# Reading expert rows back in another order at the end of a mixture-of-experts layer: picks 6 and 7 first, all tiles' sums begun with them, two pairs of rows moved from TensorE to VectorE

## The reference

```python
idx, gates = route(xf, w_router, router_bias)        # 8 of 64 experts for each of 640 tokens
hb = silu(xb @ w_gate[e]) * (xb @ w_up[e])           # for each block of rows of one expert
rows = hb @ w_down[e]
routed = segment_sum(rows * row_gate[:, None], row_tok)   # 8 gated rows summed for each token
x = x + gate * (routed + shared)                     # gate: a vector of width 1024 (g2)
y = rms_norm(x, norm_f)
```

## Time and profile before

| | us |
|---|---|
| median of 3 runs (lowest, highest) | 1039.57 (1038.82, 1041.35) |
| the profiled execution, its own time | 1040.67 |
| its span in the trace | 1038.9 |
| PE busy | 999.5 |
| DVE busy | 335.5 |
| ACT busy | 229.7 |
| POOL busy | 161.5 |
| mean rate of DMA over the span | 310 GB/s |

### The profile page before, as it was taken

One profiled execution on the slowest core, in us unless ns is written; L12 is line 12 of the kernel. 1 busy time (PEld: TensorE's weight loads), 2 busy tenths in 40 slices (PEclk: granted clock), 3 DMA queues, 4 the chain that ended last, 5 costly groups with the idle time before them and its releaser, 6 DMA issues.

```text
span 1038.9 us, 17717 instructions
## 1 busy us (share of the span) xinstructions
PE 999.5 (96%) x7077; PEld 446.7 (43%) x7077; DVE 335.5 (32%) x850; ACT 229.7 (22%) x547; POOL 161.5 (16%) x233
## 2 busy tenths in 40 slices
PE   6999999999999999999999999899999999999996
PEld 4435556565455553443333333333333333433342
DVE  1022225765236772322111111111121111112397
ACT  2131105665123240112111111111121111112111
POOL 1000010300131022112212112212122211121000
PEclk9999999999999999999999999999999999999998
DMA  9984408400101199999999999999999999999895
GB/s 324 382 333 190 162 32 231 195 2 1 62 21 41 48 403 384 402 421 419 419 421 420 419 420 389 415 420 421 418 420 415 408 360 413 419 421 384 321 410 201
DMA packets 66852, 321.62 MB, mean 310 GB/s; under 512 B 9752, under 2 KB 18608, under 8 KB 39760
## 3 DMA queue, kind: packets, MB, share of 16 engines
q1 hardware_dynamic: 50352, 272.71, 65.7%
q0 software_dynamic: 14240, 43.34, 10.5%
q10 hardware_dynamic: 2176, 4.41, 1.1%
HBM read 298.76 MB, written 31.39 MB: 318 GB/s over the span
## 4 chain that ended last, share of the span: by engine, by line
PE 87%; DMA 7%; ACT 2%; DVE 2%; issue 1%; SPq 1%; POOL 0%; ACTq 0%; POOLq 0%; DVEq 0%
PE bank L2175 30%; PE bank L2195 15%; PE bank L1937 7%; PE bank L1736 6%; DMA ring<-in_w_up 5%; PE bank L1720 4%; PE bank L2147 4%; PE bank L2031 3%; PE bank L2294 3%; PE bank L1964 2%; PE bank L2285 2%; PE bank L1950 2%; PE bank L2037 1%; PE bank L1785 1%; PE bank L1921 1%
## 5 line engine op out<-in xcount | busy, mean ns | idle before, releaser
L2175 PE MATMUL bank<-ring,reg_h 128*32 128x512 f32 x2512 | 339.7, 595 | 8.0 <-DMA ring<-in_w_up 6.1
L2175 PEld LDWEIGHTS bank<-ring,reg_h 128*32 128x32 f32 x2512 | 102.1, 110 | 194.5 <-issue 194.4
L2195 PE MATMUL bank<-ring,reg_y 128*32 128x512 f32 x1256 | 174.1, 594 | 2.8 <-ACT reg_y L1086 1.9
L2175 PE MATMUL bank<-reg_p,reg_h 128*32 128x512 f32 x624 | 126.7, 592 | 0.0
L1566 DVE TENSOR_TENSOR reg_h<-reg_p,bank 128x256 f32<-128x256 f32 x49 | 20.6, 421 | 324.0 <-ACT reg_p L1104 278.5
L1104 ACT ACTIVATE reg_p<-bank 128x256 f32<-128x256 f32 x49 | 18.8, 383 | 310.2 <-PE bank L2175 310.2
L767 POOL DMA_INDIRECT expert_rows<-reg_y,rowc x47 | 47.2, 1004 | 239.5 <-DVE reg_y L1551 229.1
L2195 PEld LDWEIGHTS bank<-ring,reg_y 128*32 128x32 f32 x1256 | 47.7, 110 | 84.9 <-issue 79.8
L1551 DVE TENSOR_SCALAR reg_y<-bank,reg_p 128x512 f32<-128x512 f32 x49 | 36.8, 751 | 131.7 <-PE bank L2195 131.7
L1937 PE MATMUL bank<-ring,reg_h 128*128 128x512 f32 x160 | 70.3, 594 | 0.0
L1093 ACT ACTIVATE reg_y<-bank,reg_p 128x512 f32<-128x512 f32 x49 | 33.7, 688 | 151.0 <-PE bank L2195 147.3
(11 more groups left out here) (294 smaller groups left out, 988.8 us busy)
## 6 DMA issues: line engine op xcount, KB each, us to landing
ring<-in_w_gate SPq DMA_DIRECT2D x51, 1024.0 KB
ring<-in_w_up SPq DMA_DIRECT2D x51, 1024.0 KB
ring<-in_w_down SPq DMA_DIRECT2D x51, 1024.0 KB
ring<-in_w_mod SPq DMA_DIRECT2D x20, 1024.0 KB, 6.4
ring<-expert_rows SPq DMA_DIRECT2D x19, 1024.0 KB, 13.7
reg_p<-in_w_gate SPq DMA_DIRECT2D x13, 1024.0 KB
reg_p<-in_w_up SPq DMA_DIRECT2D x13, 1024.0 KB
reg_p<-in_w_down SPq DMA_DIRECT2D x13, 1024.0 KB
```

The costliest lines, as they stand in the source:

```text
L2175: last = pe.matmul(bank[2 + p][R * j:R * j + R, :], xg_t[:, p, k * P + R * j:k * P + R * j + R], w_gu(homes[n % SLOTS])[:, k], start=(k == ...
L2195: last = pe.matmul(bank[y_banks(b)[hf]][R * j:R * j + R, :], h_t[:, p, i * P + R * j:i * P + R * j + R], w_dn(homes[n % SLOTS])[:, i, 512 ...
```

## The change

The requests change their order and their contents. `PART` becomes (6, 4, 2, 0): request j = 0 of a tile now holds picks 6 and 7. The j = 0 requests of all five tiles are sent first (n = 0 to 4), each into a buffer that is kept to the end; the other 15 follow tile by tile (n = 5 to 19) in the remaining seven buffers. The first five wait only for the scatters up to block 44, the sixth for all up to block 46, as the first did before. The 12 buffers are the same memory in another order. `PE_PAIRS` goes from ((3,), (3,), (1, 3), (1, 3), (1, 3)) to ((3,), (3,), (3,), (3,), (2, 3)): TensorE had 8 of the 15 later requests to add and has 6; VectorE's `more_rows` had 7 and has 9. VectorE's instructions are put in a new order. In SyncE's branch for extra groups stand two waits and an increment that do not run here.

The core of the diff (new semaphore names and the two waits in the branch are left out):

```diff
-        PART = (0, 4, 2, 6)
+        PART = (6, 4, 2, 0)
+        ACC = T
-        PE_PAIRS = ((3,), (3,), (1, 3), (1, 3), (1, 3))
+        PE_PAIRS = ((3,), (3,), (3,), (3,), (2, 3))
+        def request(t, j):
+            return t if j == 0 else ACC + 3 * t + j - 1
+        def use_of(n):
+            return (n, 0) if n < RBUF else (ACC + (n - ACC) % (RBUF - ACC), (n - ACC) // (RBUF - ACC))
...
-            sp.wait_ge(s_y, KEPT)
-            sp.wait_ge(s_yo[0], 16 * (n_even - 1))
-            sp.wait_ge(s_yo[1], groups * 64 + 16 * (n_odd - 1))
+            def rows_written(b):
+                for p in range(2):
+                    sp.wait_ge(s_yo[p], 16 * ((b - p) // 2 + 1))
             sp.wait_ge(s_zero, 32)
-            for n in range(4 * T):
-                t, j = divmod(n, 4)
-                s, value = weights_read(n) if n < RBUF else freed(n - RBUF)
+            for n, (t, j) in enumerate(REQUESTS):
+                if n == 0:
+                    rows_written(LAST[E - 1 - PART[0]])
+                if n == ACC:
+                    rows_written(KEPT - 1)
+                s, value = weights_read(n) if n < RBUF else freed(n - (RBUF - ACC))
                 sp.wait_ge(s, value)
...
+            for t in range(T - 2):
+                first_rows(t)
             gated(KEPT, 1)
-            first_rows(0)
+            for t in range(T - 2, T):
+                first_rows(t)
+            more_rows(0, 1)
             gated(KEPT + 1, 0)
-            more_rows(0, 1)
+            more_rows(0, 2)
             y_half(KEPT, 1, groups * 64 + scattered(KEPT), gate_s[:, KEPT:KEPT + 1], y_banks(KEPT)[1])
-            more_rows(0, 2)
+            more_rows(1, 1)
             y_out(KEPT + 1)
-            first_rows(1)
-            second_rows(1)
+            more_rows(1, 2)
+            more_rows(2, 1)
             joined(0)
-            for t in range(1, T - 1):
-                first_rows(t + 1)
-                finished(t - 1)
-                joined(t)
-                second_rows(t + 1)
+            more_rows(2, 2)
+            finished(0)
+            joined(1)
+            more_rows(3, 1)
+            more_rows(3, 2)
+            finished(1)
+            joined(2)
+            more_rows(4, 1)
+            finished(2)
+            joined(3)
```

More of the change, by code:

```diff
@@ L407, in build @@
         s_xw = sem("extra_weights_in")
+        s_extra = sem("extra_rows_written")
         s_oh = sem("onehots_ready")
@@ L491, in build @@
         n_even, n_odd = (NQ + 1) // 2, NQ // 2
-        PART = (0, 4, 2, 6)
+        PART = (6, 4, 2, 0)
+        ACC = T
         HOME_AT = {0: slot(3), 1: slot(0), 2: slot(1), 4: slot(2)}
-        ROWS_IN = ((4, 0), (4, 1), (4, 2), (1, 0), (1, 1), (0, 0), (0, 1), (2, 0), (2, 1), (1, 2), (0, 2), (2, 2))
-        ROWS_BY = ((s_gu, 4), (s_dn, 4), (s_piece, 4), (s_gu, 1), (s_gu, 0), (s_piece, 5), (s_piece, 6), (s_gu, 2), (s_gu, 3),
-                   (s_dn, 1), (s_dn, 0), (s_dn, 2))
-        PE_PAIRS = ((3,), (3,), (1, 3), (1, 3), (1, 3))
+        ROWS_IN = ((4, 0), (4, 1), (0, 0), (0, 1), (4, 2), (0, 2), (1, 0), (1, 1), (2, 0), (2, 1), (1, 2), (2, 2))
+        ROWS_BY = ((s_piece, 4), (s_piece, 5), (s_piece, 6), (s_piece, 7), (s_win, 0), (s_win, 1), (s_win, 2), (s_win, 3),
+                   (s_gu, 4), (s_gu, 0), (s_dn, 4), (s_dn, 0))
+        PE_PAIRS = ((3,), (3,), (3,), (3,), (2, 3))
         PE_BEFORE = tuple(sum(len(p) for p in PE_PAIRS[:t]) for t in range(T + 1))
+        DVE_PAIRS = tuple((t, j) for t in range(T) for j in (1, 2) if j not in PE_PAIRS[t])
+        def request(t, j):
+            return t if j == 0 else ACC + 3 * t + j - 1
+        REQUESTS = tuple(sorted(((t, j) for t in range(T) for j in range(4)), key=lambda tj: request(*tj)))
+        def use_of(n):
+            return (n, 0) if n < RBUF else (ACC + (n - ACC) % (RBUF - ACC), (n - ACC) // (RBUF - ACC))
         def token_rows(n):
-            h, part = ROWS_IN[n % RBUF]
+            h, part = ROWS_IN[use_of(n)[0]]
             return view(ring, HOME_AT[h] + 2048 * part, 2, D)
         def rows_in(n):
-            by, i = ROWS_BY[n % RBUF]
-            first = 16 if by is s_piece else (32 if by is s_gu else 16) * len(range(i, E, SLOTS))
-            return by[i], first + 16 * (n // RBUF + 1)
+            buf, use = use_of(n)
+            by, i = ROWS_BY[buf]
+            first = 16 if by is s_piece or by is s_win else (32 if by is s_gu else 16) * len(range(i, E, SLOTS))
+            return by[i], first + 16 * (use + 1)
         def weights_read(n):
@@ L517, in freed @@
         def freed(n):
-            t, j = divmod(n, 4)
-            if j == 0:
-                return s_fr, t + 1
+            t, j = REQUESTS[n]
             if j in PE_PAIRS[t]:
                 return s_tp, PE_BEFORE[t] + PE_PAIRS[t].index(j) + 1
-            return s_du, t + 1
+            return s_du, DVE_PAIRS.index((t, j)) + 1
         KEPT = NQ - 2
@@ L1633, in first_rows @@
             def first_rows(t):
-                rows = token_rows(4 * t)
-                dve.wait_ge(*rows_in(4 * t))
+                rows = token_rows(t)
+                dve.wait_ge(*rows_in(t))
                 link(dve.tensor_tensor(rows[:, 0, :], rows[:, 0, :], rows[:, 1, :], ALU.add))
             def more_rows(t, j):
-                half, rows = token_rows(4 * t)[:, 0, :], token_rows(4 * t + j)
-                dve.wait_ge(*rows_in(4 * t + j))
+                half, rows = token_rows(t)[:, 0, :], token_rows(request(t, j))
+                dve.wait_ge(*rows_in(request(t, j)))
                 link(dve.tensor_tensor(half, half, rows[:, 0, :], ALU.add))
[L1642 to L1652, removed]
+                dve.tensor_tensor(half, half, rows[:, 1, :], ALU.add).then_inc(s_du, 1)
+                dve.wait_ge(s_du, DVE_PAIRS.index((t, j)) + 1)
             def joined(t):
-                half = token_rows(4 * t)[:, 0, :]
+                half = token_rows(t)[:, 0, :]
                 dve.wait_ge(s_tp, PE_BEFORE[t + 1])
@@ L2287, in _ @@
                 for j in PE_PAIRS[t]:
-                    n = 4 * t + j
+                    n = request(t, j)
                     pe.wait_ge(*rows_in(n))
```

6 lines of the change are left out of this document (4 added, 2 removed).

## The result

The changed kernel takes 1043.2 us (median of 12 runs, 1041.29 to 1045.07), the kernel before, beside it, 1040.67 (12 runs, 1038.82 to 1041.86). The ratio is 1.0025, with 1.0016 to 1.0035 as its 95% interval: 2.5 us slower, under 0.3%, but clear of no change. The profiled execution took 1041.29 us, 1.9 us less than the median, with a span of 1039.5.

What follows compares the result with a forecast made beforehand. TensorE's sums bound the kernel before; after, row landings were to hold tile 0's `joined` to 999.2, plus 39.3 of VectorE's chain: 1038.5 against 1035.8, 2.6 us later. On the median that gave 1042.2 us, range 1037 to 1045.

Steps and rivals of the forecast that it cites:

- sixth request: Row request that block 48's product on VectorE stands behind; forecast to land at 981.4 us.
- block 48's product done: VectorE's product, behind the sixth request's two adds; forecast done at 984.3 us, against 976.76 in the kernel before.
- ninth request: Tile 1's pair on VectorE, ahead of `y_out`; forecast to land at 989.0 us.
- twelfth request: Tile 2's pair on VectorE, ahead of tile 0's `joined`; forecast to land at 996.7 us.
- S, tile 0's `joined`: Start of tile 0's `joined` on VectorE, after the twelfth request's adds; forecast at 999.2 us, break-even 996.6.
- from S to the end: VectorE's chain from tile 0's `joined` through the last tile, summed from timeline steps to 39.3 us.
- TensorE's wait for block 48's product: TensorE was to stand still 3.9 us ahead of its transposes, its down product ending at 988.9 us.
- The k-th landing by 966.0 + 2.56k: Rows follow the slowest DMA engine's old work, one request per 2.56 us; 3.9 us of supply gained; chance 0.48.
- So no gap is added here: The first five requests' waits for block 44's scatter and block 46's down product were to add no gap.
- A lag that isn't carried: Rival: lagging DMA engine catches up, landings move 6.8 us, twelfth request at 993.8, time 1039.3 us; chance 0.18.
- a bound by VectorE alone: Rival: rows do not bind, tile 0's `joined` starts near 992.1, gain 4.4 us, time 1035.2 us; chance 0.12.
- The slower rival: Slowest DMA engine falls further behind, deciding from 0.5 us on; at 2 us the time is 1044.2; chance 0.22.

Runs made afterwards that it cites:

- late: Changed kernel with the first five row requests held until all scatters have landed; ratio 1.0064 to the kernel before.
- hold: Changed kernel with the first five row requests held some 6 us, until block 46's output is copied to `yb`; ratio 1.0028 to the kernel before.
- half: Changed kernel with the first five row requests at half size, pick 7 of every token not read; ratio 1.0017 to the kernel before.
- reorder: Changed kernel with VectorE's order altered: block 48's product, output copies and tile 0's `joined` ahead of pairs of adds; ratio 1.0021 to the kernel before.
- pair back: Changed kernel with only tile 3's second pair given back to TensorE, which then adds 7 requests; ratio 1.0026 to the kernel before.
- traffic: Kernel before plus two unused 1 MB weight loads, issued once block 44's scatter has landed; 1042.5 us, one execution.
- e1_late: Changed kernel with the first five row requests waiting for all 47 scatters like the rest; ratio 1.0064 to the kernel before.

## Why the prediction was right, and where it was not

By its steps, all from the anchor (956.35 in its sum, 954.48 in the profile after), a landing being read as the start of the add that waited for it:

| step | predicted, us | measured, us |
|---|---|---|
| sixth request | 25.05 | 24.98 |
| block 48's product done | 27.95 | 27.92 |
| ninth request | 32.65 | 32.45 |
| twelfth request | 40.35 | 40.20 |
| S, tile 0's `joined` | 42.85 | 42.71 |
| from S to the end | 39.3 | 39.25 |
| TensorE's wait for block 48's product | 3.9 | 0.29 |

- *The size.* The difference was forecast as 2.6 us and measured as 2.5. The 1042.2 us was counted from a median of three runs that lay 1.1 us below that of twelve, which is why the time itself came out 1.0 higher.
- *The supply.* The k-th landing by 966.0 + 2.56k held within 0.25 us for the eight that VectorE waited for (the first six, the ninth, the twelfth). The late run puts the worth of the early start at 3.4 us on the twelfth, and the hold run shows that the time of issue doesn't matter while the backlog lasts. The Trainium skill, "DMA: Bandwidth & Descriptors", section "Queues, rings and completion order", has a ring for each pair of queue and engine; these landings agree with it. Which engines lag, and why by 8 us, no run here shows. The start of the formula is less well founded than its fit: the packets of the earlier trace rows that end at 965.6 are all of the scatters' queue, the only queue with packets in 965 to 966.2, and the weights' queue, behind which the rows stand, starts its last packet before 965.0. So 965.6 was not read from the backlog that it was to stand for, and that it fits so well is in part luck. The line of the DMA queues before, 965 to 966.2:

```profile
q0 software_dynamic: 4, 0.01, 2.5%
```

- *VectorE's chain*, 39.3 us, was right as a sum of rows, and in `half` it is 39.24 again (995.61 to 1034.85).
- *TensorE was wrong.* The step that failed is the one on the five early requests, "So no gap is added here". It looked at SyncE's and GpSimd's waits and not at what their traffic does to TensorE. The stop behind block 46's down product was 3.87 us instead of 1.88, and the 65 records behind it took 9.15 us instead of 7.46, at a granted clock of one half. That made TensorE 3.7 us late (1.99 + 1.69), and so its wait for block 48's product nearly vanished. That the two take each other's place was not foreseen, and they did it with 0.29 us to spare: block 48's down product ended 32.6 us from the anchor (987.12), as forecast (988.9 - 956.35), but for another reason. The end didn't see it: the twelfth request set S either way, which the hold run shows (stop 2.01, wait 3.71, length the same). It does cost when the rows are taken off the path: 1.38 us of waiting in `reorder`, and in `half` the twelfth request's buffer opens late.
- *The rivals.* A lag that isn't carried would have put the twelfth request at 37.5 from the anchor (993.8 - 956.35), and a bound by VectorE alone would have started `joined` at 35.8 (992.1 - 956.35). They came at 40.2 and 42.7. The slower rival wanted a landing 0.5 us later than forecast; the sixth, the ninth and the twelfth were 0.1 to 0.2 earlier.
- *Why the stop grows* is shown down to one packet and argued from there. At the stop TensorE passes the branch for extra groups, which is not taken. In each of the twelve kernels one packet of 16 KB of the instruction queue starts 2.7 to 2.8 us before TensorE goes on (its start read in steps of 0.05 us). In the seven with the short stop (before, `late`, `hold` and the four built on `hold`) it starts 2.8 to 2.9 us from the anchor, while the down product still runs; in the five with the long stop it starts 4.75 to 5.4 us from it, when the product (3.64 us) has ended. The packet itself takes 0.92 us either way. So the growth of the stop against the kernel before, 2.0 to 2.6 us, goes with this packet's later start, 1.95 to 2.6 us, beside full DMA engines. DMA queues (packets, MB, share of 16 engines) of 959.1 to 960.2 before, then of 959.2 to 960.2 in the change:

```profile
q8 instruction: 1, 0.02, 5.3%
```
```profile
q1 hardware_dynamic: 49, 0.22, 53.7%
q0 software_dynamic: 42, 0.17, 43.5%
q8 instruction: 1, 0.02, 5.8%
```

In the change it is one packet among 91 of rows and scatters. The Trainium skill, "Runtime: NRT & Kernel Launch", section "Instruction fetch mechanics", has code fetched in blocks of 16 KiB over a DMA queue that the sequencer drives, and a stall where a taken branch leaves the loaded pages. This branch isn't taken, so the page doesn't say what is seen here; that TensorE waits for the code in this packet, and that the queues beside it delay it, fits all twelve kernels but was not tested apart from the traffic.

## What to carry to other kernels

When a transfer is to start earlier, ask what the slowest DMA engine still has to do, not what the mean share leaves free: of 6.8 us of free rate 3.4 to 4.0 were to be had, and shifting the issue by 6.4 us changed nothing. Traffic put where DMA was quiet may cost on an engine that moves no data, so look at every stop of that engine in the window; here it was one at a branch. Where single edits each give nothing, read what waits next after each: here three limits stood within 3 us of one another, and only together did the edits turn 1.0025 into 0.9973.

## What the runs showed of the hardware that I had not expected

- TensorE's stop behind block 46, at the branch, was 1.88 to 2.01 us in the seven kernels in which DMA moved 76 to 85 GB/s during it, and 3.87 to 4.46 us in the five in which it moved 361 to 402 GB/s (the change, reorder, pair back, half, traffic).
- The 65 records behind each of those five long stops took 8.87 to 9.15 us instead of 7.46, and the granted clock behind them was 0.50 to 0.52 (2 us windows). Single stops of 2.54, 2.97 and 3.71 us were followed by down products of 4.87, 5.38 and 5.38 us instead of 3.64 to 3.69 (`e1_late`, `e2_hold`). In the run with block 48's product earlier, the clock was at 0.58 and 0.50 around two stops of 2.15 and 1.87 us, while behind the single stops of 1.88 to 2.01 us the 65 records took their 7.46 us.
